# Down products of inner tiles 0 to 15 as seven quarter products, over sums of inner quarters

## The chip, the cores and the metric

The kernel runs on one core of one Trainium2 chip. The metric is the device time of one execution, in microseconds (us), the median of several runs. Its engines are called PE (matmuls; PEld are its weight loads), DVE, ACT, POOL and SP (which issues the weight DMAs).

## What is computed

Two transformer blocks in float32 on 512 tokens of width 1024. Three places are feed-forward networks (FFN) with an inner width of 2816, one in the first block and two in the second; everything between them (projections, attention, mixers) is left as it is by this change.

```python
def first_block(...):
    ...
    hn = rms_norm(h, norm2_g)
    gate, up = jnp.split(hn @ w_gate_up, 2, axis=-1)
    h = h + (jax.nn.silu(gate) * up) @ w_down        # FFN 0
    return rms_norm(h, final_g)[:, N_META:]
def second_block(...):
    x = x + 0.5 * swiglu(rms_norm_2(x, ffn1_norm), w_gate, w_up, w_down)   # FFN 1
    ...
    x = x + 0.5 * swiglu(rms_norm_2(x, ffn2_norm), w_gate, w_up, w_down)   # FFN 2
    x = x + sigmoid(rms_norm_2(x, ple_norm) @ w_ple_gate) * (p @ w_ple_proj)
```

## The kernel before

Activations lie transposed: the 1024 channels are 8 tiles of 128 partitions, the 512 tokens are columns. A float32 product is made of three float32r passes, high x high, high x low and low x high (`passes`, L791). So each weight chunk (`raw`, up to 128x2048) is split: ACT writes the rounded high part (`whi`), POOL the rest (`wlo`), both in two slots, and activations have high and low parts as well (`xh`, `xl`; inner ones `fh`, `fl`, a ring of 9 tiles).

An FFN is a line of 34 chunks (`PLACES`): "up" chunks, one for each of the 22 inner tiles (gate and up weights for 128 inner channels), and "down" chunks, four in each of three rounds r, each adding to two output tiles of `hT`. The rounds take 6, 8 and 8 inner tiles (`DOWN_K`) and stand behind 7, 8 and 7 up chunks (`UPS`). The places are called p = 0 to 33 here.

Up chunks of inner tiles 4 to 21 are folded (`fold_chunk`, L932): the 2x2 block product (two halves of the 1024 inputs, gate and up columns, two halves of the tokens) is made with seven quarter products of 256 columns instead of eight, which is 7 x 4 x 3 = 84 matmuls of 256 columns in place of 48 of 512. The seven, P0 to P6 in the order in which PE runs them, need sums of weight quarters (`corner_sums`, `sums_low`, on DVE, through PSUM banks 1, 3, 5, 7), sums of activation quarters (`fsh`, `fsl`, made once an FFN by `fold_sums`) and copies of partial results between them: ACT's three `kept` copies (`prod_kept`) before P2, P3 and P4, DVE's `up_done` additions before P5 and P6. Down chunks are plain: `down_chunk`, L975, 3 matmuls of 512 columns for each inner and output tile.

Everything is ordered by hand. Each engine has its own `ffn(f, ...)` loop over p and waits on counting semaphores. In place p, ACT makes the high parts of chunk p+1 (`coming`, in four steps between its other work), POOL their low parts, DVE finishes chunk p-1 and adds up chunk p+1's quarters. In the last round each finished output tile is fed to the next norm at once (`feed`): ACT scales and squares it (L1355, L1363, for FFN 0 a second square, L1373, since a norm with the final gain follows first), DVE writes the low part (`split`) and adds the squares (`add_square`, L1907, and L1915). POOL's loop, whose order matters for the change, is in its core

```python
for p in range(1, FFN_LEN):
    if folded(p + 1):
        fold_low(f, p + 1)
        continue
    ...
    if p + 1 < FFN_LEN:
        low(C_F[f] + p + 1)
```

and begins an FFN with `low(C_F[f])` and `low(C_F[f] + 1)`, the low parts of its first two chunks. A plain chunk on PE waits for its own `low` (`w_lo`), and the first chunk after an FFN waits for the squares' sum between its matmuls (`norm_sums`, L897; for FFN 1 between its two output tiles).

Of the kernel before, what the change touches and what calls it, by code (L numbers as in the profile page):

```python
# [47 lines left out]
DOWN_K = (6, 8, 8)  # L48
UPS = (7, 8, 7)
# [78 lines left out]

def folded(p):

    return up_tile(p) is not None and up_tile(p) >= PLAIN


def fold_no(f, p):

    return (FK - PLAIN) * f + up_tile(p) - PLAIN
# [22 lines left out]
def build(nc, I, out):  # L159
    with ExitStack() as ctx:  # L160
# [50 lines left out]
        fsh = at("fsh", 0, [P, 4, 4 * FOLD + 8], F32R)[:, :, 0:4 * FOLD].rearrange("p n (k t) -> p n k t", k=4)  # L211
        fsl = at("fsl", 4128, [P, 4, 4 * FOLD + 8], F32R)[:, :, 0:4 * FOLD].rearrange("p n (k t) -> p n k t", k=4)
        fh = at("fh", 8320, [P, RING, T], F32R)
        fl = at("fl", 12928, [P, RING, T], F32R)
        foldh = at("foldh", 17536, [P, 6, 4 * P + 8], F32R)[:, :, 0:4 * P].rearrange("p (s u) n -> p s u n", s=2)
        foldl = at("foldl", 20656, [P, 6, 4 * P + 8], F32R)[:, :, 0:4 * P].rearrange("p (s u) n -> p s u n", s=2)
        tmp = at("tmp", 23808, [P, 4, T])
        low_sum = at("low_sum", 25856, [P, 4, P])
        prod1 = at("prod1", 26368, [P, FOLD])
        prod5 = at("prod5", 26624, [P, FOLD])  # L220
        prod6 = at("prod6", 26880, [P, FOLD])
# [121 lines left out]
        silu_done, h_done, h_hi, h_split = sem("silu_done"), sem("h_done"), sem("h_hi"), sem("h_split")  # L343
# [84 lines left out]
        def corner(n, a, b):  # L428

            return raw[:, n % 2, :].rearrange("p (k n) -> p k n", k=DK)[:, 4 * a:4 * a + 4, P * b:P * b + P]  # L430
# [5 lines left out]
        def unit(c, n):  # L436

            if n < 4:
                return whi[:, c % 2, 4 * P * n:4 * P * n + 4 * P], wlo[:, c % 2, 4 * P * n:4 * P * n + 4 * P]
            return foldh[:, c % 2, n - 4, :], foldl[:, c % 2, n - 4, :]  # L440
# [4 lines left out]
        def fold_out(c):  # L445

            return ps[:, bank(c, 0), FOLD:T], ps[:, bank(c, 1), 0:FOLD], ps[:, bank(c, 1), FOLD:T]

# [8 lines left out]
        def _(sp):  # L457
# [26 lines left out]
            def ffn(f, gate, up, down):  # L484
                for p in range(FFN_LEN):
                    c = C_F[f] + p
                    if up_tile(p) is not None:
                        s, sel = slot(c, DK, CW), slice(P * up_tile(p), P * up_tile(p) + P)
                        load(c, [(s[:, :, 0:P], gate[:, :, sel]), (s[:, :, P:CW], up[:, :, sel])])
                    else:  # L490
# [120 lines left out]
        def _(pool):  # L611
# [49 lines left out]
            def ffn(f):  # L661
                low(C_F[f])
                low(C_F[f] + 1)
                for p in range(1, FFN_LEN):
                    if folded(p + 1):
                        fold_low(f, p + 1)
                        continue
# [1930 lines left out]
```

## Time and profile before

| what | us |
|---|---|
| median of 3 runs (lowest, highest) | 1967.1 (1965.23, 1967.56) |
| the profiled execution, its own time | 1966.0 |
| its span, first to last instruction | 1964.2 |
| PE busy | 1946.3 (99%) |
| DVE, POOL, ACT busy | 1197.6, 1134.5, 931.3 |
| share of PE in the chain that ended last | 88% |

Each row of the timeline below gives start, duration, engine, line, operation, output<-input, shapes and count; in brackets the time for which the engine had waited and for whom. A matmul's duration covers its way through the pipeline, so the pace of PE is read from starts and from stretches, not from durations. The 128x512 in a row is partitions x columns.

### The profile page before, as it was taken

Reading aid. Unit: us, or ns where it says so; the run is one execution under the profiler, and the core shown is the slowest. Engines: PE = TensorE matmul, PEld = TensorE weight load, DVE = VectorE, ACT = ScalarE, POOL = GpSimd, SP = SyncE. Lnnn points to the kernel's source line nnn. Section 1 sums busy time; section 2 is a strip of 40 time slices with the busy share of each in tenths; the row PEclk is TensorE's granted clock in tenths of the full one; section 3 lists DMA queues with packets and bytes.
Section 4 is the critical chain, followed back from the end, with each engine's and each line's share of the span. In section 5 each row is a group of like instructions: output and inputs, shape, how many; then the busy total and the mean of one; then the engine's idle time right before and its main releaser. Section 6 shows DMA issues by size and latency. Waiting matters only on the chain.

```text
span 1964.2 us, 30689 instructions
## 1 busy us (share of the span) xinstructions
PE 1946.3 (99%) x11449; PEld 1719.8 (88%) x11449; DVE 1197.6 (61%) x2067; ACT 931.3 (47%) x1649; POOL 1134.5 (58%) x915
## 2 busy tenths in 40 slices
PE   9999999999999999999999999999999999999999
PEld 8998887888899989879998988889888888999977
DVE  6588665635647455775755656677645565646574
ACT  6413225533536435454552644667644463634532
POOL 5344442254667657557775756666554566766663
PEclk9999999999999999999999999999999999999999
DMA  5222331123333333323333332332222333333331
GB/s 179 91 87 91 102 94 56 44 86 107 87 108 103 113 86 108 102 71 108 108 108 88 107 108 87 107 101 79 77 89 86 94 94 106 106 113 91 108 109 75
DMA packets 253850, 189.68 MB, mean 97 GB/s; under 512 B 6608, under 2 KB 249680, under 8 KB 253680
## 3 DMA queue, kind: packets, MB, share of 16 engines
q1 hardware_dynamic: 253024, 187.53, 32.0%
q8 instruction: 87, 1.43, 0.3%
q14 instruction: 51, 0.42, 0.1%
q10 hardware_dynamic: 688, 0.31, 0.1%
HBM read 180.93 MB, written 2.10 MB: 93 GB/s over the span
## 4 chain that ended last, share of the span: by engine, by line
PE 88%; DVE 5%; ACT 3%; issue 3%; POOL 1%; DMA 0%; DVEq 0%; SPq 0%; ACTq 0%
PE ps L793 18%; PE ps L794 18%; PE ps L795 18%; PE ps L944 9%; PE ps L945 9%; PE ps L946 9%; PE ps L1133 1%; PE ps L1285 1%; DVE tmp L1891 1%; ACT whi L1350 1%; PE ps L1205 1%; PE ps L1206 1%; PE ps L1207 1%; DVE hT L2076 1%; PE ps L1273 1%
## 5 line engine op out<-in xcount | busy, mean ns | idle before, releaser
L631 POOL TENSOR_TENSOR wlo<-raw,whi 128x512 fp32r<-128x512 f32 (+2 forms) x420 | 547.2, 1335 | 532.2 <-ACT whi L1350 411.3
L793 PE MATMUL ps<-xh,whi 128*128 128x512 f32 (+1 forms) x1008 | 380.3, 377 | 1.7 <-POOL wlo L631 1.7
L795 PE MATMUL ps<-xh,wlo 128*128 128x512 f32 (+1 forms) x1008 | 372.9, 370 | 0.0
L794 PE MATMUL ps<-xl,whi 128*128 128x512 f32 (+1 forms) x1008 | 372.7, 370 | 0.0
L1350 ACT ACTIVATE whi<-raw 128x2048 fp32r<-128x2048 f32 (+1 forms) x86 | 160.8, 1869 | 335.5 <-PE ps L795 287.1
L654 POOL TENSOR_TENSOR wlo<-raw,whi 128x512 fp32r<-128x512 f32 x162 | 213.2, 1318 | 152.6 <-ACT whi L1404 152.4
L793 PEld LDWEIGHTS ps<-xh,whi 128*128 128x128 f32 x1008 | 189.5, 188 | 33.4 <-POOL wlo L631 2.5
L795 PEld LDWEIGHTS ps<-xh,wlo 128*128 128x128 f32 x1008 | 189.3, 188 | 33.0
L794 PEld LDWEIGHTS ps<-xl,whi 128*128 128x128 f32 x1008 | 189.9, 188 | 28.4 <-issue 0.7
L793 PE MATMUL ps<-fh,whi 128*128 128x512 f32 x528 | 205.9, 390 | 1.6 <-POOL fl L643 1.6
L794 PE MATMUL ps<-fl,whi 128*128 128x512 f32 x528 | 205.6, 389 | 0.0
L795 PE MATMUL ps<-fh,wlo 128*128 128x512 f32 x528 | 205.4, 389 | 0.0
L1404 ACT ACTIVATE whi<-raw 128x512 fp32r<-128x512 f32 x162 | 102.0, 633 | 160.0 <-PE ps L946 102.4
L2001 DVE TENSOR_TENSOR foldl<-ps,foldh 128x512 fp32r<-128x512 f32 x162 | 108.2, 688 | 31.0 <-ACT foldh L1408 29.9
L944 PE MATMUL ps<-fsh,whi 128*128 128x256 f32 x432 | 121.7, 282 | 3.4 <-ACT prod L1462 3.4
L946 PE MATMUL ps<-xh,wlo 128*128 128x256 f32 x432 | 122.0, 282 | 0.0
L945 PE MATMUL ps<-xl,whi 128*128 128x256 f32 x432 | 121.9, 282 | 0.0
L944 PE MATMUL ps<-xh,whi 128*128 128x256 f32 x432 | 121.9, 282 | 0.0
L946 PE MATMUL ps<-fsh,wlo 128*128 128x256 f32 x432 | 121.5, 281 | 0.0
L945 PE MATMUL ps<-fsl,whi 128*128 128x256 f32 x432 | 121.5, 281 | 0.0
L944 PE MATMUL ps<-fsh,foldh 128*128 128x256 f32 x432 | 121.4, 281 | 0.0
L946 PE MATMUL ps<-fsh,foldl 128*128 128x256 f32 x432 | 121.4, 281 | 0.0
(385 smaller groups left out, 4900.1 us busy)
## 6 DMA issues: line engine op xcount, KB each, us to landing
raw<-in_w_in SPq DMA_DIRECT2D x87, 512.0 KB, 4.5
raw<-in_w_gate_up SPq DMA_DIRECT2D x44, 512.0 KB, 5.0
raw<-in_ffn_w_gate SPq DMA_DIRECT2D x44, 512.0 KB, 4.0
raw<-in_ffn_w_up SPq DMA_DIRECT2D x44, 512.0 KB, 5.3
raw<-in_ffn_w_down SPq DMA_DIRECT2D x32, 512.0 KB, 4.3
raw<-in_w_down SPq DMA_DIRECT2D x16, 512.0 KB, 4.1
raw<-in_ffn_w_down SPq DMA_DIRECT2D x16, 384.0 KB, 3.4
raw<-in_w_b SPq DMA_DIRECT2D x8, 512.0 KB, 3.9
```

The source lines that it names most:

```text
L631: ins = pool.tensor_tensor(wlo[:, c % 2, cs], raw[:, c % 2, cs], whi[:, c % 2, cs].bitcast(F32), ALU.subtract)
L654: pool.tensor_tensor(by_k(lo), corner(c, a, b), by_k(hi).bitcast(F32), ALU.subtract).then_inc(raw_lo, 1)
L793: pe.matmul(o, w_of(whi), xhi, start=first, stop=False)
L794: pe.matmul(o, w_of(whi), xlo, start=False, stop=False)
L795: return pe.matmul(o, w_of(wlo), xhi, start=False, stop=last)
L944: pe.matmul(o, wh[:, ks], hi[:, k, :], start=first and k == 0, stop=False, skip_group_check=True)
L945: pe.matmul(o, wh[:, ks], lo[:, k, :], start=False, stop=False, skip_group_check=True)
L946: mm = pe.matmul(o, wl[:, ks], hi[:, k, :], start=False, stop=k == 3, skip_group_check=True)
L1133: mm = pe.matmul(o[:, first:T], ctok[:, q, :], pT[:, q, first:T], start=q == 0, stop=False)
L1350: act.activation(whi[:, c % 2, 0:n], raw[:, c % 2, 0:n], ACT.Copy).then_inc(w_hi, 1)
L1404: act.activation(by_k(unit(c, u)[0]), corner(c, a, b), ACT.Copy).then_inc(raw_hi, 1)
L2001: dve.tensor_tensor(lo, ps[:, 3 + 2 * m, :], hi.bitcast(F32), ALU.subtract).then_inc(sum_lo, 1)
```

## The change

- `DOWN_K` becomes 8, 8, 6 and `UPS` 9, 8, 5: rounds 0 and 1 now take eight inner tiles each (0 to 15), behind one more up chunk than they need, and round 2 takes the last six.
- The eight down chunks of rounds 0 and 1 are folded too: 84 matmuls of 256 columns over inner tiles 2i (first half) and 2i+1 (second half) and the two halves of the tokens. Round 2 stays plain, with 36 matmuls of 512 columns a chunk instead of 48.
- New sums of inner quarters, for each pair of tiles i = 0 to 7, in two stages (`f_sums`, `f_lows` on DVE, `f_forms` on ACT), at the places that `FORM_STEPS` gives: one stage in each of two places, except i = 3 and i = 7, whose two stages stand in one place (p = 8 and p = 20). Their high and low parts lie in `fs24h`, `fs24l` and in halves of `fh`, `fl`, `xh`, `xl` that are free; SP moves one of them by two small DMAs.
- In an up chunk the addition `up_done` is made once, behind P4, and in PSUM; the inner tile is then made from PSUM in two halves. `low_sum`, `prod1`, `prod6` are gone (their places are `raw` itself and `tmp`).
- The quarter sums of weights use bank 3 twice, so that bank 7 is free for the inner sums; the third now waits for the first one's low part.
- The update of `hT` reads the scaled product from PSUM, not from `tmp`.
- FFN 1: the multiplication of `hT` by the final gain and norm, on DVE in round 0 before, is made by ACT (`gain_done`) and POOL (`xn_done`) in places 3 to 10.
- FFN 0, round 2: seven of the eight additions of squares go from DVE to POOL.

```diff
-DOWN_K = (6, 8, 8)
-UPS = (7, 8, 7)
+DOWN_K = (8, 8, 6)
+UPS = (9, 8, 5)
...
+    return up_tile(p) is not None and up_tile(p) >= PLAIN or down_part(p) is not None and down_part(p)[0] < 2
...
+FORM_STEPS = {}
+for _i in range(DK):
+    _p = UP_AT[2 * _i + 1] + 1
+    FORM_STEPS.setdefault(_p, []).append((_i, 0))
+    FORM_STEPS.setdefault(_p if _i % 4 == 3 else _p + 1, []).append((_i, 1))
...
@@ gpsimd, ffn
+                    if f == 0 and down_part(p) is not None:
+                        for m in fed(p):
+                            pool.wait_ge(sq_done, 2 * DK + m + 1)
+                            pool.wait_ge(ssum_done, 19 + m)
+                            pool.tensor_tensor(ssum[:, META:TM], ssum[:, META:TM], sq[:, META:TM], ALU.add).then_inc(ssum_done, 1)
...
@@ vector, ffn
+            def f_sums(f, i, stage):
+
+                a, b, s = slice(0, FOLD), slice(FOLD, T), ps[:, 7, :]
+                dve.wait_ge(fs_lo, form_level(f, i, stage) - 1)
+                if stage == 0:
+                    dve.wait_ge(acc_free, 2 * (C_F[f] + UP_AT[2 * i + 1]) + 2)
+                    dve.tensor_tensor(s[:, a], f_t[0][:, a], f_t[1][:, a], ALU.add)
+                    dve.tensor_tensor(s[:, b], f_t[0][:, b], f_t[0][:, a], ALU.subtract).then_inc(fs_sum, 1)
+                else:
+                    link(dve.tensor_tensor(s[:, b], s[:, b], f_t[1][:, a], ALU.subtract))
+                    dve.tensor_tensor(s[:, a], s[:, b], f_t[1][:, b], ALU.add).then_inc(fs_sum, 1)
...
+                    for i, stage in steps[:1]:
+                        f_sums(f, i, stage)
                     if new:
+                        sums_low(f, p + 1, 0)
                         corner_sums(f, p + 1, 2)
-                        sums_low(f, p + 1, 0)
+                    for i, stage in steps[:1]:
+                        f_lows(f, i, stage)
+                    for i, stage in steps[1:]:
+                        f_sums(f, i, stage)
+                    if new:
                         sums_low(f, p + 1, 1)
...
-                        dve.wait_ge(prod_done, 5 * m + 4)
-                        dve.wait_ge(prod_kept, 3 * m + 3)
-                        dve.wait_ge(h_done, FK * f + up_tile(p))
-                        dve.tensor_tensor(tmp[:, 2, FOLD:T], r5, prod6[:], ALU.add).then_inc(up_done, 1)
+                        dve.wait_ge(prod_done, 5 * m + 5)
+                        dve.wait_ge(prod_kept, 3 * m + 2)
+                        dve.tensor_tensor(fold_up(c), r1, prod5[:], ALU.add).then_inc(up_done, 1)
...
-                        stt(tmp[:, 2, :], ps[:, bank(c, t), :], factor, rsx, ALU.mult, ALU.mult).then_inc(acc_free, 1)
-                        dve.tensor_tensor(x, x, tmp[:, 2, :], ALU.add).then_inc(h_new, 1)
+                        link(stt(o, o, factor, rsx, ALU.mult, ALU.mult))
+                        link(dve.tensor_tensor(x, o, x, ALU.add))
+                        feed(S + 1, m, gain, own_square=not (S + 1 == 2 and m < DK - 1))
```

POOL at the end of FFN 0 and the start of FFN 1 (`wlo<-raw,whi` is the low part of a chunk, `fl` that of an inner tile, `ssum<-ssum,sq` an addition of squares). Before, from the last inner tile's low part in FFN 0 on:

```order
136 L631 TENSOR_TENSOR wlo<-raw,whi 128x512 x4
137 L643 TENSOR_TENSOR fl<-tmp,fh 128x512 x2
138 L631 TENSOR_TENSOR wlo<-raw,whi 128x512 x24
139 L643 TENSOR_TENSOR fl<-tmp,fh 128x512
140 L631 TENSOR_TENSOR wlo<-raw,whi 128x512 x4
```

After:

```order
162 L704 TENSOR_TENSOR wlo<-raw,whi 128x384 x4
163 L717 TENSOR_TENSOR fl<-rt,fh 128x512
164 L717 TENSOR_TENSOR fl<-sq,fh 128x512
165 L704 TENSOR_TENSOR wlo<-raw,whi 128x384 x4
166 L759 TENSOR_TENSOR ssum<-ssum,sq 128x512
167 L704 TENSOR_TENSOR wlo<-raw,whi 128x384 x4
168 L759 TENSOR_TENSOR ssum<-ssum,sq 128x512 x2
169 L704 TENSOR_TENSOR wlo<-raw,whi 128x384 x4
170 L759 TENSOR_TENSOR ssum<-ssum,sq 128x512 x4
171 L704 TENSOR_TENSOR wlo<-raw,whi 128x512 x12
```

The seven additions stand between the low parts of the down chunks; the last four, for output tiles 3 to 6, stand ahead of row 171, whose first four are the low part of FFN 1's first chunk.

DVE in one folded up chunk, p = 8 of FFN 0, where both stages of i = 3 stand (`ps<-rt,sq`, `ps<-rt`, `ps<-ps,sq` are the sums, `xl<-ps,xh`, `fl<-ps,fh` and `fs24l` their low parts; `ps<-ps,prod` is the addition for which P6 waits). Before, a folded up chunk was:

```order
592 L2013 TENSOR_TENSOR tmp<-ps,rs 128x256
593 L1988 TENSOR_TENSOR ps<-ps,raw 128x512
594 L1991 TENSOR_TENSOR ps<-ps,raw 128x512
595 L2023 TENSOR_TENSOR tmp<-tmp 128x512
596 L1994 TENSOR_TENSOR ps<-ps,raw 128x512
597 L2001 TENSOR_TENSOR foldl<-ps,foldh 128x512 x2
598 L2041 TENSOR_TENSOR tmp<-ps,prod_59 128x256
599 L2001 TENSOR_TENSOR foldl<-ps,foldh 128x512
600 L2045 TENSOR_TENSOR tmp<-ps,prod_58 128x256
```

After, from the inner tile's product on:

```order
656 L2194 TENSOR_TENSOR sq<-tmp,ps 128x256
657 L2195 TENSOR_TENSOR sq<-tmp,ps 128x256
658 L2121 TENSOR_TENSOR ps<-rt,sq 128x256
659 L2122 TENSOR_TENSOR ps<-rt 128x256
660 L2158 TENSOR_TENSOR sum_l<-ps,sum_h 128x512
661 L2151 TENSOR_TENSOR ps<-ps,raw 128x512
662 L2133 TENSOR_TENSOR xl<-ps,xh 128x256
663 L2133 TENSOR_TENSOR fl<-ps,fh 128x256
664 L2124 TENSOR_TENSOR ps<-ps,sq 128x256
665 L2125 TENSOR_TENSOR ps<-ps,sq 128x256
666 L2158 TENSOR_TENSOR sum_l<-ps,sum_h 128x512
667 L2229 TENSOR_TENSOR ps<-ps,prod_60 128x256
```

Six new operations of 256 columns stand ahead of row 667.

## Rows read from the trace of the kernel before

**Rows 1.** The page: span, busy time, granted clock in tenths by slice.

```profile
span 1964.2 us, 30689 instructions
...
PE 1946.3 (99%) x11449; PEld 1719.8 (88%) x11449; DVE 1197.6 (61%) x2067; ACT 931.3 (47%) x1649; POOL 1134.5 (58%) x915
...
PEclk9999999999999999999999999999999999999999
```

**Rows 2.** Stretches of FFN 0: from:to us, then length, busy us (count) of each engine.

```profile
531.94:561.84 29.90, 29.90 (x253) 29.89 (x252) 14.47 (x27) 15.83 (x34) 20.46 (x17) 1.00 0.36 107
...
594.51:674.75 80.24, 79.98 (x674) 79.80 (x672) 51.18 (x91) 46.42 (x97) 59.28 (x47) 1.00 0.38 107
...
674.75:718.29 43.54, 43.54 (x194) 36.04 (x193) 18.69 (x22) 11.85 (x14) 24.07 (x18) 1.00 0.32 99
```

**Rows 3.** Timeline of PE: the longest wait at a folded chunk.

```profile
951.86 0.35 PE L944 MATMUL ps<-fsh,whi 128*128 128x256 f32 x1 [2.41 <-ACT prod L1462]
```

**Rows 4.** Waits of PE from 480 us on: for whom, us, times, longest.

```profile
PE ps L944 <- ACT prod L1462: 3.4, 6, 2.4
PE ps L910 <- DVE ssl L1926: 2.6, 2, 1.3
PE ps L793 <- POOL wlo L631: 1.7, 2, 1.0
```

**Rows 5.** Timeline: FFN 0's last tiles and the first chunk of FFN 1.

```profile
822.28 1.92 ACT L1350 ACTIVATE whi<-raw 128x2048 fp32r<-128x2048 f32 x1
...
824.28 4.85 POOL L631 TENSOR_TENSOR wlo<-raw,whi 128x512 fp32r<-128x512 f32 x3 [4.41 <-ACT whi L1350]
...
826.20 1.77 DVE L1907 TENSOR_TENSOR ssum<-ssum,sq 128x512 f32<-128x512 f32 x1
...
829.09 1.74 POOL L631 TENSOR_TENSOR wlo<-raw,whi 128x512 fp32r<-128x512 f32 x1
...
829.60 0.68 DVE L1891 SCALAR_TENSOR_TENSOR tmp<-ps,rs 128x512 f32<-128x512 f32 x1
...
832.05 0.62 ACT L1363 ACTIVATE sq<-hT 128x512 f32<-128x512 f32 x1
...
832.92 0.68 DVE L1907 TENSOR_TENSOR ssum<-ssum,sq 128x512 f32<-128x512 f32 x1
...
832.90 0.39 PE L793 MATMUL ps<-xh,whi 128*128 128x512 f32 x1
...
841.23 0.79 PE L793 MATMUL ps<-xh,whi 128*128 128x512 f32 x1
```

**Rows 6.** Timeline: FFN 2's last round and the chunk behind it.

```profile
1859.32 0.40 PE L793 MATMUL ps<-fh,whi 128*128 128x512 f32 x1
...
1864.81 0.50 PE L793 MATMUL ps<-fh,whi 128*128 128x512 f32 x1 [0.54 <-POOL fl L643]
...
1903.75 0.39 PE L793 MATMUL ps<-xh,whi 128*128 128x512 f32 x1
...
1912.71 0.50 PE L910 MATMUL ps<-ssh,ones 128*128 128x512 f32 x1 [1.32 <-DVE ssl L1926]
```

**Rows 7.** Groups by line: busy us, mean ns of one.

```profile
L652 POOL TENSOR_TENSOR low_sum<-raw 128x512 f32<-128x512 f32 x54 | 70.6, 1307 | 0.0
...
L631 POOL TENSOR_TENSOR wlo<-raw,whi 128x384 fp32r<-128x384 f32 x48 | 52.1, 1116 | 38.1 <-ACT whi L1350 28.3 <-ACT whi L1395 9.8
```

**Rows 8.** Timeline: DVE and ACT in a folded chunk that PE begins at 634.80.

```profile
639.71 0.40 ACT L1462 ACTIVATE prod<-ps 128x256 f32<-128x256 f32 x1
...
640.78 0.43 DVE L2041 TENSOR_TENSOR tmp<-ps,prod 128x256 f32<-128x256 f32 x1 [0.63 <-PE ps L946]
```

**Rows 9.** Timeline: FFN 1, places 2 to 4.

```profile
869.99 0.50 PE L793 MATMUL ps<-xh,whi 128*128 128x512 f32 x1 [0.98 <-POOL wlo L631]
...
880.92 0.68 DVE L2056 TENSOR_TENSOR tmp<-ps,rs 128x512 f32<-128x512 f32 x1
...
882.66 0.39 ACT L1462 ACTIVATE prod<-ps 128x256 f32<-128x256 f32 x1 [0.28 <-PE ps L946]
```

More of the change, by code:

```diff
@@ L935, in fold_chunk, with product @@
                 r1, r5, r2 = fold_out(c)
-                k1, k2 = slice(0, 4), slice(4, DK)
-                late = slice(META + FOLD, TM)
-                early = slice(META, META + FOLD)
-                def product(o, u, hi, lo, first=True, last=True):
-                    wh, wl = unit(c, u)
+                late, early = slice(FOLD, T), slice(0, FOLD)
+                part = down_part(p)
+                def product(o, u, rows, first=True):
+                    wh, wl = unit(f, p, u)
                     for k in range(4):
@@ L943, in product @@
                         ks = slice(P * k, P * k + P)
[L944 to L950 removed]
+                        hi, lo = rows(k)
@@ new lines, in product, with form, quarter, rows @@
+                        pe.matmul(o, wh[:, ks], hi, start=first and k == 0, stop=False, skip_group_check=True)
+                        pe.matmul(o, wh[:, ks], lo, start=False, stop=False, skip_group_check=True)
+                        mm = pe.matmul(o, wl[:, ks], hi, start=False, stop=k == 3, skip_group_check=True)
+                    return mm
+                def form(m):
+                    return lambda k: x_form(m, k) if part is None else f_form(part[0], m, k)
+                def quarter(second, half):
+                    def rows(k):
+                        if part is None:
+                            cs = slice(META + half.start, META + half.stop)
+                            return xh[:, 4 * second + k, cs], xl[:, 4 * second + k, cs]
+                        z = (DK * part[0] + 2 * k + second) % RING
+                        return fh[:, z, half], fl[:, z, half]
+                    return rows
@@ new lines, in ffn @@
+                    kept(tmp[:, 0, 0:FOLD], r1, 3)
+                    for i in FORMS_AT[f == 1].get(p, ()):
+                        x_forms(f, i, own)
+                    steps = FORM_STEPS.get(p, [])
+                    for i, stage in steps[:1]:
+                        f_forms(f, i, stage)
+                    coming(3)
+                    for i, stage in steps[1:]:
+                        f_forms(f, i, stage)
+                    if f == 1 and p - PLAIN + 1 in range(DK):
+                        m = p - PLAIN + 1
+                        act.wait_ge(fs_sum, form_level(f))
+                        act.activation(hT[:, m, META:TM], hT[:, m, META:TM], ACT.Copy, scale=col(vec, V_FIN + m)).then_inc(gain_done, 1)
```

344 lines of the change are left out of this document (220 added, 124 removed).

## The prediction

> **What bounds the kernel now.** I read the page first. PE is busy for 1946.3 of 1964.2 us and its granted clock is full in all forty slices [rows 1]; no other engine is above 61%. So the time is PE's: the matmuls that it has, at their pace, and its few waits. The stretches of FFN 0 give the pace: three folded chunks 29.90, eight 80.24, four plain down chunks with eight inner tiles 43.54 [rows 2]. That is 9.97 to 10.03 for a folded chunk and 10.885 for a plain one. Then the list of PE's waits: 3.4 us in six waits for ACT's copy `prod`, one of them 2.41, each in the first folded chunk after a down round [rows 3, 4]; the rest are small. The reader is to see that a change can gain only PE time or these waits, and that DVE (6.4 us in a folded up chunk of 10.03), ACT (5.8) and POOL (7.4) have a third or less to spare before they set the pace themselves [rows 2].
>
> The profiled execution took 1966.0, 1.1 below the median of 1967.1. I sum changes against it and apply the same sum to the median.
>
> **1. Cheaper matmuls.** Each FFN had four down chunks with six tiles and eight with eight; now eight with eight tiles are folded and four with six are plain. So 24 chunks go from 10.885 to 9.99 us, 84 matmuls of 256 columns for 48 of 512: 24 x 0.895 = **-21.5**. This is certain as long as PE is fed.
>
> **2. Waits that go.** No folded chunk follows a plain down chunk any more, and the scaling of `hT` in FFN 1 leaves DVE's round 0, behind which the 2.41 stood. All six waits go: **-3.4** [rows 3, 4]. At the low end none but the 2.41 goes.
>
> **3. DVE inside a folded down chunk.** Its work is two updates of `hT` of two operations each, six sums, the addition before P6 and one more of 512 columns. In steps of 0.6 to 0.7 us for 512 columns and 0.4 for 256 (the 0.43 and 0.68 of [rows 8, 5]) this is about 8 us of 9.99. It fits, and PE's P6 waits for an addition that can start, as now, 0.3 us behind P4's end, 1.42 us ahead of P6. ACT's third copy ends at 640.11, PE wants it at 634.80 + 4 x 1.42 = 640.5 [rows 8]; new work stands behind it. Price 0 in the steady case, hidden by that slack of 0.4; what it costs without it is the slower rival.
>
> **4. Both stages of i = 3 and i = 7 in one place.** In an ordinary up chunk the new sums add four operations of 256 columns ahead of the addition for P6, about 1.7 us, or 2.7 where the two with both inputs in SBUF run beside POOL. DVE had some 3 us idle [rows 2], and by my count the addition is ready 0.6 us early. In p = 8 and p = 20 six operations stand there, and it is 0.3 to 0.4 late. 6 x 0.35 = **+2.1**, between 0 and 6 x 1 us.
>
> **5. Start of FFN 1.** Its activation sums are made in places 1 and 2, so DVE is late: the gate product of place 3 starts at 880.92, and ACT's copy in the first folded chunk is made at 882.66, 1.2 us ahead of need (883.87, PE's third product) [rows 9]. The stages (0,0) and (0,1) put about 2.4 and 1.6 us ahead of that product, 1.1 of idle time goes, and ACT's new scaling adds 0.5. The copy comes at 885.7: **+1.9**, between 0 and 3. FFN 0 and 2 begin less densely and have some 3 us to spare there. The 0.98 wait [rows 9] stays.
>
> **6. End of FFN 1 and FFN 2.** Round 2 is shorter by 4 x 2.72 = 10.9 us on PE, but not on DVE. From its start to the norm's matmul was 1912.71 - 1859.32 = 53.39 [rows 6]; with 10.9 less it would be 42.5. Now follow DVE. The last inner tile's low part ended 5.49 us behind the round's start [rows 6]; ACT's shorter high part ahead of it saves 0.3, and the first output tile is done at 5.9 (4.08 without the wait, which was 0.54 and is now 1.8). Each output tile then costs DVE: product 0.72, update 0.73, 0.83 until ACT's high part is there, low part 0.67, addition 0.60, together 3.55. Beside POOL the last two take 1.1 and 1.7, 5.1 in all; one tile of each two is so, since POOL has four operations of 1.1 for each chunk [rows 7], and the addition shows both times, 1.77 and 0.68 [rows 5]. Two tiles are 8.65 against PE's 8.16. Eight tiles from 6.1 on, with 0.8 of early waits, end at 41.5, the split of the sum (3.1) at 44.6. That is 2.1 over 42.5, **+4.2** for both, between 2 and 7.
>
> POOL, by the Trainium skill (GPSIMD Engine Reference, 1. Specifications), shares its SBUF interfaces with DVE, and contends with DVE instructions that have two SBUF inputs. The trace agrees: 1.77 beside POOL, 0.68 without. It speaks for the updates of `hT`, which read PSUM now, and against the additions that move to POOL.
>
> **7. End of FFN 0.** Here is the largest loss. DVE gives seven additions of squares to POOL, where the last four stand ahead of the low part of FFN 1's first chunk. Today ACT has that chunk's high part ready at 824.20, POOL lowers it from 824.28 to 830.83, PE needs it at 832.90 [rows 5]: 2.07 us of cover. In the new order POOL cannot begin before it has added the square of output tile 6. When is that? DVE's tile costs product and update 1.45, then it waits for ACT's second square (scale, square, square: 1.9 us behind the update), then the second sum's addition, 0.6 alone and up to 1.7 beside POOL, which now adds in just that moment: 3.95 to 5.05, and I take 4.9. PE's tile takes 4.08. Tile 6's product starts at 6.1 + 6 x 4.9 = 35.5 behind the round's start, its square is there 3.07 later (829.60 to 832.67) [rows 5], 38.6, POOL's addition takes 1.3 [rows 7], 1.6 beside DVE, 40.2, the low part 5.2 to 6.5 [rows 5, 7], say 6.3: 46.5. PE has ended the round at 34.5, so it waits 12.0. Add 0.9 for the wait at the round's start as in 6, take off 1.0 for waits inside that chunk (832.90 to 841.23 is 8.33 us [rows 5]) that have been served by then: **+11.9**. With 3.95 a tile it is 6.5; with every operation slow, 14.5.
>
> **8. After an idle time of 12 us.** The longest idle time in the rows is 2.41, and behind it a matmul took 0.35 in place of 0.28 [rows 3]; at that the clock stayed full [rows 1]. What 12 us do is not shown. Bounds: nothing, or the whole next pass of 24 matmuls of 0.227 at the lower level of 1.2 GHz, twice the time, 5.4. I take **+2.0**, nearer to the row.
>
> Sum: -21.5 - 3.4 + 2.1 + 1.9 + 4.2 + 11.9 + 2.0 = **-2.8** or, with the roundings, -2.9. That is 1963.1 for an execution like the profiled one and **1964.2 for the median**.
>
> **The rivals.**
>
> A. The boundary behind FFN 0 costs no more than the other two (2.1), because DVE and ACT run closer to 3.95 a tile and POOL finds time early. For it: 2.07 us of cover today [rows 5]. Against: the order has no way around, tile 6's square comes after the moment at which the low part now begins. -2.8 - 9.8 - 2.0 = -14.6, 1952.5.
>
> B. The clock falls in the 12 us and takes its whole price, 5.4 in place of 2.0: +3.4, 1967.6. The rows neither show nor exclude it. The Trainium skill (TensorE: Matmul & The Clock Gate, The HAM clock gate) says that the array falls to half rate after an idle window and must be busy to get back; by that rule part of the following pass is slow, and no row here has such an idle time.
>
> C. Slower than before: the folded chunk no longer fits DVE and ACT. Place: ACT's third copy ahead of P4, 0.4 us of slack [rows 8]. In a folded down chunk DVE ends its second update of `hT` about 0.65 behind the next chunk's first need, ACT's sums wait for DVE's, and the copy waits behind them. From 0.4 more on, PE waits in each of the 24 chunks; with 0.5 each it is +12, 1976.2. Against it: round 2's operations on PSUM and the sums show 0.6 to 0.7 each, and my count leaves 0.4.
>
> **How the numbers follow.** Forecast 0.52, A 0.16, B 0.17, C 0.15. About 0.2%, 3.9 us, is what a measurement of this kernel can tell from no change. The forecast's own range is 1957 to 1970, with the ends of terms 4 to 8 set against each other, and its middle lies near the border at 1963.2: 0.24 faster, 0.27 the same, 0.01 slower. A is faster. B gives 0.02 faster, 0.13 the same, 0.02 slower. C is slower. Sum: faster 0.42, same 0.40, slower 0.18. The range takes in the forecast, B, part of A and of C: 1955 to 1974.
>
> **What would show it.** A folded down chunk's 84 matmuls at 10.0 us and no waits in the steady ones (1, 3). In p = 8 and 20 a wait of some 0.3 at P6 for DVE (4). In FFN 1's p = 4 a wait at the third product for ACT (5). Norm sums of the last two FFNs 44.6 behind the round's start (6). One wait of PE of about 12 us for `wlo` at FFN 1's first chunk, with four additions of `ssum` in front on POOL, and the granted clock behind it (7, 8). I am wrong if that wait is under 6 us, or if PE waits in most folded down chunks.

## The result, and the profile after

The changed kernel takes **2095.9 us** (median of 4 runs, 2090.7 to 2099.2) against 1967.0 of the kernel before: 1.0655 times as long, 95% interval 1.0643 to 1.0668. The prediction was 1964.2, range 1955 to 1974, with 0.18 on slower. It was wrong by 132 us, nearly all of it in one term.

The page of the changed kernel, to be read beside [rows 1]: PE was busy for 99% of the span and is for 94% now. Of the chain of work that ended last, PE had 88% before; it has 69% now, and DVE and ACT have 24%.

```profile
span 2088.6 us, 33448 instructions
...
PE 1953.5 (94%) x12313; PEld 1758.1 (84%) x12313; DVE 1372.0 (66%) x2412; ACT 1042.3 (50%) x1951; POOL 1156.0 (55%) x954
...
PE 69%; DVE 17%; ACT 7%; issue 6%; POOL 1%; DMA 0%; DVEq 0%; ACTq 0%; SPq 0%; POOLq 0%
```

PE's waits in the changed kernel, for whom, us in total, times, longest. They answer to [rows 4]:

```profile
PE ps L1030 <- ACT tmp L1578: 107.2, 76, 3.0
PE ps L879 <- POOL wlo L704: 12.4, 3, 11.1
PE ps L879 <- POOL fl L717: 4.6, 3, 1.5
PE ps L879 <- DVE xl L2025: 1.8, 2, 1.5
PE ps L996 <- DVE ssl L2061: 1.7, 2, 0.8
...
PE ps L1030 <- DVE ps L2229: 0.3, 2, 0.2
```

The first row is new and is nearly everything: 76 waits in 78 folded chunks, the up chunks that were folded already among them, nearly all of them before P4 for ACT's third kept copy (L1578). The other rows are about what was forecast. The stretches of FFN 0, to be read beside [rows 2] (from:to, length, busy us of PE, PEld, DVE, ACT, POOL, granted clock):

```profile
531.83:837.38 305.55, 270.25 (x2185) 265.95 (x2184) 210.85 (x355) 160.72 (x339) 186.18 (x149) 0.98 0.32 91
837.38:883.21 45.83, 33.20 (x146) 26.78 (x144) 31.41 (x37) 25.27 (x32) 30.09 (x25) 0.93 0.24 70
```

26 folded chunks take 305.55 us, 11.75 each, where 26 x 9.99 = 259.7 were expected. With FFN 1 (304.1) and FFN 2 (303.1) that is 133 us too much, more than the whole loss of 124.4 between the two spans.

**Why the copy is late.** The changed kernel in the folded down chunk whose P4 PE starts at 625.13 (start, duration, engine, line, operation; in brackets how long the engine had waited, and for whom), ACT and PE first, then DVE:

```profile
622.02 0.60 ACT L1516 ACTIVATE sum_h<-ps 128x512 fp32r<-128x512 f32 x1 [0.20 <-DVE ps L2148]
624.11 0.60 ACT L1516 ACTIVATE sum_h<-ps 128x512 fp32r<-128x512 f32 x1 [1.49 <-DVE ps L2151]
624.61 0.38 ACT L1578 ACTIVATE tmp<-ps 128x256 f32<-128x256 f32 x1
...
625.13 0.35 PE L1030 MATMUL ps<-fh,whi 128*128 128x256 f32 x1 [0.90 <-ACT tmp L1578]
```

```profile
622.65 0.69 DVE L2158 TENSOR_TENSOR sum_l<-ps,sum_h 128x512 fp32r<-128x512 f32 x1 [0.66 <-ACT sum_h L1516]
623.38 0.70 DVE L2151 TENSOR_TENSOR ps<-ps,raw 128x512 f32<-128x512 f32 x1
```

Read the two as one line. ACT makes the high part of the first sum (622.02). DVE waits for it, writes its low part (622.65), then makes the third sum (623.38), and only then ACT may make the high part of the *second* sum (624.11): `sum_high(m)` waits for `3 * n + min(m + 2, 3)` sums, which for m = 1 is all three. The kept copy is queued behind it. In the kernel before, the third sum stood ahead of the first low part and ended at 638.25, before ACT came to its second copy, so ACT made both in one go (new rows, of before, for the chunk of [rows 8]):

```profile
637.56 0.69 DVE L1994 TENSOR_TENSOR ps<-ps,raw 128x512 f32<-128x512 f32 x1
...
638.24 1.08 ACT L1408 ACTIVATE foldh<-ps 128x512 fp32r<-128x512 f32 x2
```

The diff exchanged these two lines on DVE, since bank 3 holds the first sum until its low part is made and the third sum now goes there. It left ACT's wait as it was.

**Where it is 2.7 us.** In an up chunk in which stage 0 stands, DVE is late as well (changed kernel, DVE, then ACT and PE):

```profile
678.32 1.54 DVE L2121 TENSOR_TENSOR ps<-rt,sq 128x256 f32<-128x256 f32 x1
679.78 1.52 DVE L2122 TENSOR_TENSOR ps<-rt 128x256 f32<-128x256 f32 x1
681.21 0.68 DVE L2158 TENSOR_TENSOR sum_l<-ps,sum_h 128x512 fp32r<-128x512 f32 x1
681.92 0.70 DVE L2151 TENSOR_TENSOR ps<-ps,raw 128x512 f32<-128x512 f32 x1
```

```profile
682.65 0.60 ACT L1516 ACTIVATE sum_h<-ps 128x512 fp32r<-128x512 f32 x1 [3.11 <-DVE ps L2151]
...
684.19 0.36 PE L1030 MATMUL ps<-xs13h,whi 128*128 128x256 f32 x1 [2.73 <-ACT tmp L1578]
```

Two sums of 256 columns take 1.5 us each; stage 1's, of the same size but with one operand in PSUM, take 0.43. I had priced both at some 0.95, and only in p = 8 and 20 did I count their delay.

### The profile page after: what moved, and what is told of

Read it like the earlier page. It is cut to its first block, busy times and chain, and to the rows that moved or that the text cites. A ratio compares the mean times of both kernels' runs of the same rounds, so it can differ in the third digit from the quotient of the medians.

```text
span 2088.6 us, 33448 instructions
## 1 busy us (share of the span) xinstructions
PE 1953.5 (94%) x12313; PEld 1758.1 (84%) x12313; DVE 1372.0 (66%) x2412; ACT 1042.3 (50%) x1951; POOL 1156.0 (55%) x954
## 4 chain that ended last, share of the span: by engine, by line
PE 69%; DVE 17%; ACT 7%; issue 6%; POOL 1%; DMA 0%; DVEq 0%; ACTq 0%; SPq 0%; POOLq 0%
PE ps L879 13%; PE ps L880 12%; PE ps L881 12%; PE ps L1030 8%; PE ps L1032 8%; PE ps L1031 8%; DVE ps L2025 2%; DVE ps L2151 2%; DVE sum_l L2158 2%; DVE ps L2145 2%; ACT fh L1600 2%; DVE ps L2122 1%; DVE ps L2121 1%; ACT tmp L1578 1%; PE ps L1239 1%
## 5 line engine op out<-in xcount | busy, mean ns | idle before, releaser
L704 POOL TENSOR_TENSOR wlo<-raw,whi 128x512 fp32r<-128x512 f32 (+2 forms) x324 | 410.0, 1297 | 428.8 <-ACT whi L1456 330.6
L730 POOL TENSOR_TENSOR wlo<-raw,whi 128x512 fp32r<-128x512 f32 x234 | 303.5, 1298 | 345.2 <-ACT whi L1510 345.2
L1510 ACT ACTIVATE whi<-raw 128x512 fp32r<-128x512 f32 x234 | 147.9, 632 | 174.7 <-PE ps L1032 174.0
L1516 ACT ACTIVATE sum_h<-ps 128x512 fp32r<-128x512 f32 x234 | 140.2, 599 | 154.9 <-DVE ps L2151 150.0
L2158 DVE TENSOR_TENSOR sum_l<-ps,sum_h 128x512 fp32r<-128x512 f32 x234 | 159.8, 684 | 68.8 <-ACT sum_h L1516 68.8
L1030 PE MATMUL ps<-xs13h,whi 128*128 128x256 f32 x216 | 66.0, 306 | 82.1 <-ACT tmp L1578 82.1
L728 POOL TENSOR_TENSOR raw<-raw 128x512 f32<-128x512 f32 x78 | 104.7, 1342 | 0.0
L830 POOL TENSOR_TENSOR wlo<-raw,whi 128x384 fp32r<-128x384 f32 (+1 forms) x84 | 75.6, 931 | 51.4 <-ACT whi L1920 50.7
L1030 PE MATMUL ps<-fh,whi 128*128 128x256 f32 x288 | 83.1, 289 | 22.1 <-ACT tmp L1578 22.1
L735 POOL TENSOR_TENSOR wlo<-raw,whi 128x512 fp32r<-128x512 f32 x78 | 101.1, 1296 | 0.0
L1030 PE MATMUL ps<-xh,sum_h 128*128 128x256 f32 x312 | 88.2, 283 | 0.6 <-DVE ps L2229 0.3
```

What stands on the lines that cost most here:

```text
L704: ins = pool.tensor_tensor(wlo[:, c % 2, cs], raw[:, c % 2, cs], whi[:, c % 2, cs].bitcast(F32), ALU.subtract)
L730: pool.tensor_tensor(by_k(lo), corner(f, p, a, b), by_k(hi).bitcast(F32), ALU.subtract).then_inc(raw_lo, 1)
L1030: pe.matmul(o, wh[:, ks], hi, start=first and k == 0, stop=False, skip_group_check=True)
L1510: act.activation(by_k(unit(f, p, u)[0]), corner(f, p, a, b), ACT.Copy).then_inc(raw_hi, 1)
L1516: act.activation(unit(f, p, 4 + m)[0], ps[:, (3, 5, 3)[m], :], ACT.Copy).then_inc(sum_hi, 1)
L2158: dve.tensor_tensor(lo, ps[:, (3, 5, 3)[m], :], hi.bitcast(F32), ALU.subtract).then_inc(sum_lo, 1)
```

## The experiments

All compared with the kernel before on the same chip, in three rounds. A diff is against the changed kernel unless it says otherwise, and "+ e1" means that the edit stands on top of experiment 1.

### 1. Both copies together

```diff
-                    act.wait_ge(corner_sum, 3 * n + min(m + 2, 3))
+                    act.wait_ge(corner_sum, 3 * n + (2, 2, 3)[m])
...
                     dve.wait_ge(sum_lo, 3 * n + 1)
+                    dve.wait_ge(sum_hi, 3 * n + 2)
                     dve.tensor_tensor(sums(3), sums(5), corner(f, p, 1, 0), ALU.add).then_inc(corner_sum, 1)
```

> The changed kernel; ACT's second copy of a sum no longer waits for the third sum, and DVE's third sum waits for that copy instead (so bank 5 is still read by one engine at a time). Theory A (ACT's third kept copy is late because the copy ahead of it waits behind DVE's low part and third sum): the wait of 0.9 or 2.7 us before P4 goes in nearly all of the 78 folded chunks; 107 us of listed waits and some 20 of what they bring behind them go, 1965 to 1985 us. DVE's addition before P6 may now be the next to be late in the chunks with stage 0. Theory B (DVE as a whole is too full in chunks with stage 0, the copy is only where it shows): the 0.9 waits go, the 24 of 2.7 us move to P6 at about 2 us each: 2010 to 2030. Theory C (the folded chunk is slower for another reason, the waits are filled by something else): above 2060.

Measured: **1966.2 us**, ratio 1.0002 (0.9992 to 1.0011). Two waits moved, and 130 us are gone: theory A. The time is 2 us above the 1964.2 that I had forecast for the change; how far that is luck is said below. PE's waits in this kernel:

```profile
PE ps L879 <- POOL wlo L704: 12.4, 3, 11.1
PE ps L1030 <- DVE ps L2230: 6.9, 7, 1.0
PE ps L879 <- POOL fl L717: 4.6, 3, 1.5
...
PE ps L1030 <- ACT tmp L1578: 1.2, 1, 1.2
```

ACT's copy is late once, at FFN 1's start. DVE's addition before P6 is now late 1.04 us in each p = 8 and p = 20, six times, which the waits before P4 had covered in the changed kernel (0.17 twice).

The second wait is there so that ACT's copy and DVE's third sum don't read bank 5 together. No run here shows what would come of that; the Trainium skill (PSUM — Partial Sum Buffer, PSUM bank collisions raise a hardware error) says that two engines may not touch one bank at once, reads included.

### 2. The exchange alone, in the kernel before

```diff
@@ the kernel before
-                        corner_sums(f, p + 1, 2)
                         sums_low(f, p + 1, 0)
+                        corner_sums(f, p + 1, 2)
                         sums_low(f, p + 1, 1)
```

> The kernel before with one thing of the change alone: DVE makes the low part of the first sum ahead of the third sum, not behind it. Theory A: ACT's second copy of a sum waits for both, about 2 us later than now, its third kept copy ends near 1.2 us behind PE's need, in each of 54 folded chunks: +65 to +80, 2030 to 2050 us. If the order of these two is not the cause: within 5 us of the kernel before.

Measured: **2027.9 us**, ratio 1.031 (1.030 to 1.033). The exchange of two lines costs the kernel before 62 us, with nothing else of the change in it:

```profile
PE ps L944 <- ACT prod L1462: 51.9, 45, 4.7
```

It is a little under the expected 2030: I had counted 54 chunks, and the list has 45. The last chunk of each of the nine runs of folded ones has no such wait, since no folded chunk follows it whose sums DVE and ACT would have to prepare in it.

### 3. The third copy first

```diff
                     coming(2)
+                    kept(tmp[:, 0, 0:FOLD], r1, 3)
+                    coming(4)
                     if n is not None:
...
-                    kept(tmp[:, 0, 0:FOLD], r1, 3)
```

`coming(2)` makes only the first sum's high part here, and a new step, `coming(4)`, the second's.

> The changed kernel; only ACT's order differs: its third kept copy stands ahead of the second copy of a sum and of the inner tile's high part, all waits as they were. Theory A: PE no longer waits before P4, about 1965 to 1985 us, close to the kernel in which the two copies stand together. Theory B: as there, 2010 to 2030. If ACT's amount of work were the cause, not the wait in front of the copy, then the copy would be as late as before in the chunks without a wait and the time would stay above 2060.

Measured: **2024.2 us**, ratio 1.028 (1.027 to 1.030). A miss. The wait before P4 went in all steady chunks, so ACT's amount of work was not the cause; but it came back at P6 in the chunks with stage 0. ACT's second copy still waits 2.17 us for DVE's third sum, and what stands behind it on ACT, stage 0's two copies, is late for DVE, in whose queue the addition for P6 stands behind them (DVE, then PE):

```profile
672.24 0.42 DVE L2135 TENSOR_TENSOR xl<-ps,xh 128x256 fp32r<-128x256 f32 x1 [1.73 <-ACT fh L1552]
672.58 0.41 DVE L2135 TENSOR_TENSOR fl<-ps,fh 128x256 fp32r<-128x256 f32 x1
672.91 0.68 DVE L2160 TENSOR_TENSOR sum_l<-ps,sum_h 128x512 fp32r<-128x512 f32 x1
673.51 0.42 DVE L2231 TENSOR_TENSOR ps<-ps,prod 128x256 f32<-128x256 f32 x1
```

```profile
674.08 0.42 PE L1030 MATMUL ps<-xh,sum_h 128*128 128x256 f32 x1 [1.94 <-DVE ps L2231]
```

So moving the late copy forward treats the place where the wait shows. Only taking away the detour over DVE (1) helps.

### 4. Stage 0 with one operand from PSUM

```diff
-                    dve.tensor_tensor(s[:, a], f_t[0][:, a], f_t[1][:, a], ALU.add)
-                    dve.tensor_tensor(s[:, b], f_t[0][:, b], f_t[0][:, a], ALU.subtract).then_inc(fs_sum, 1)
+                    dve.tensor_tensor(s[:, a], s[:, a], f_t[1][:, a], ALU.add)
+                    dve.tensor_tensor(s[:, b], s[:, b], f_t[0][:, a], ALU.subtract).then_inc(fs_sum, 1)
```

> The changed kernel; the two sums of stage 0 read one operand from PSUM (bank 7) in place of the one in SBUF, so the sums of inner quarters are not the right ones; count, shapes and order of all instructions are kept. Theory: the price of 1.54 and 1.52 us is that of two operands in SBUF beside POOL's work; with one in PSUM each takes about 0.42, the wait before P4 in the 24 chunks with stage 0 falls from 2.7 to about 0.9: -45 to -50, 2045 to 2055 us, while the waits of 0.9 stay. Rival: POOL's work slows any operation of DVE at that place: they stay near 1.5 and the time near 2096.

Measured: **2052.1 us**, ratio 1.043 (1.042 to 1.045).

```profile
PE ps L1030 <- ACT tmp L1578: 76.1, 75, 3.0
```

The 18 waits of 2.73 us are 1.11 now, the 0.9 waits stay. So with the detour in place stage 0's two operands in SBUF cost some 44 of the 129 us (31 of them in the list of waits, some 9 in the clock behind long waits, below). The two shares don't simply add: experiment 1 takes away the detour alone and gets all 130 back, since without it the same slow sums mostly fit into DVE's slack.

### 5. What makes two operands in SBUF slow: POOL's instruction in halves (+ e1)

```diff
                     pool.wait_ge(raw_hi, 3 * n + z + 1)
-                    pool.tensor_tensor(by_k(lo), corner(f, p, a, b), by_k(hi).bitcast(F32), ALU.subtract).then_inc(raw_lo, 1)
+                    for k in (slice(0, 2), slice(2, 4)):
+                        ins = pool.tensor_tensor(by_k(lo)[:, k], corner(f, p, a, b)[:, k], by_k(hi)[:, k].bitcast(F32), ALU.subtract)
+                    ins.then_inc(raw_lo, 1)
```

> The kernel with both copies together (e1); POOL makes the low parts of the first three weight quarters of a folded chunk in two instructions of 256 columns each in place of one of 512. In the trace of e1 the two sums of stage 0 (256 columns, 1.54 and 1.53 us) end 0.3 us behind POOL's two operations that run at that time (574.27 for 1.29, 575.51 for 1.49). Theory L: DVE's operation with two operands in SBUF does not run slowly beside POOL's, it waits for the end of POOL's instruction and then takes 0.3. Then the first of the two falls to about 1.0 or less, the waits of 1.04 at P6 shrink or go: 1959 to 1963. Theory S: the two share the memory's ports by the element, and an instruction's length doesn't matter: both stay near 1.5 us, and the time at 1966 or, as POOL's own work grows by some 0.7 a chunk, up to 1 above.

Measured: **1956.3 us**, ratio 0.9947 (0.9930 to 0.9964), 9.9 below experiment 1, although POOL has more to do. In quarters (four slices of one k each):

> The kernel with both copies together (e1), with POOL's low parts of the first three weight quarters in four instructions of 128 columns each. Theory L (DVE's operation with two operands in SBUF waits for the end of POOL's running instruction): the first sum of stage 0, 1.54 us beside instructions of 512 columns and 0.99 beside those of 256, is near 0.7 here. If instead a halved POOL instruction merely let DVE in after a fixed time, it stays at 0.99. The time: as e7, 1956 to 1958, or higher by what POOL's greater work costs, since a quarter's low part then takes some 1.9 us and P3 waits for it if that is late.

Measured: 1963.0 us (1959.6 to 1966.2), ratio 0.9982 (0.9973 to 0.9992). The same place, the end of p = 8's inner tile in FFN 0, with POOL's instructions whole, halved and quartered (experiment 1, then 5, then quarters; DVE's sum and POOL's instructions beside it):

```profile
574.31 1.54 DVE L2121 TENSOR_TENSOR ps<-rt,sq 128x256 f32<-128x256 f32 x1
...
574.27 1.29 POOL L730 TENSOR_TENSOR wlo<-raw,whi 128x512 fp32r<-128x512 f32 x1 [0.47 <-ACT whi L1510]
```

```profile
574.06 0.99 DVE L2123 TENSOR_TENSOR ps<-rt,sq 128x256 f32<-128x256 f32 x1
...
574.02 1.62 POOL L731 TENSOR_TENSOR wlo<-raw,whi 128x256 fp32r<-128x256 f32 x2 [0.34 <-ACT whi L1512]
```

```profile
573.62 0.72 DVE L2123 TENSOR_TENSOR ps<-rt,sq 128x256 f32<-128x256 f32 x1
...
572.24 3.44 POOL L731 TENSOR_TENSOR wlo<-raw,whi 128x128 fp32r<-128x128 f32 x7
```

One POOL instruction takes 1.29, 0.75 and 0.47 us (the means of these groups over the FFNs are 1297, 750 and 470 ns), DVE's sum 1.54, 0.99 and 0.72: each time 0.25 more than POOL's. The ends say it more sharply: of the 48 sums of stage 0 in each of these three traces 40, 38 and 42 took over 0.5 us, and every one of them ended 0.29 or 0.30 us behind the end of a POOL instruction; the others, with POOL idle or just ending, took 0.42 to 0.50. The sum does not run slowly beside POOL; it stands still until a POOL instruction ends, then does its own work. The Trainium skill says so (SBUF — State Buffer, SBUF: two separate sides): the port pair that DVE and POOL share is an exclusive lock held for a whole instruction, and a DVE operation with two SBUF inputs needs it where the POOL operation reads SBUF. The trace agrees, with these three pairs; I had cited a softer sentence of another page and priced a mean slowdown.

The gain of 9.9 is more than the six waits of 1.04. In experiment 1 the up chunks with stage 0 took 10.25 us and the others 9.91, a stop at P6 too short for the list of waits; in halves nearly all take 9.91. In quarters the steady chunks do too, but one wait of 3.9 us for DVE's addition stands in the list of the profiled run, and the runs spread over 6.5 us.

The trace shows what makes that wait, and halves have it as well. At one place, p = 6 of FFN 1, POOL has work without a pause, and DVE's sum is not let in behind the first of POOL's instructions but only behind the last (the kernel with halves, DVE, then POOL):

```profile
908.95 3.59 DVE L2123 TENSOR_TENSOR ps<-rt,sq 128x256 f32<-128x256 f32 x1
```

```profile
908.11 2.88 POOL L731 TENSOR_TENSOR wlo<-raw,whi 128x256 fp32r<-128x256 f32 x4
910.89 1.36 POOL L728 TENSOR_TENSOR raw<-raw 128x512 f32<-128x512 f32 x1
```

Four POOL instructions end while the sum stands, and it takes 3.59 us; in quarters, at the same place, ten do and it takes 5.73. With whole instructions POOL waited for ACT between them there, and the sum took 1.54. PE's wait for the addition behind it is 1.06 in halves and 3.87 in quarters. The whole 6.7 us between the two kernels are not explained by that, as only one execution of each was profiled. Nor is it shown what decides whether DVE is let in between two POOL instructions: elsewhere it was, between two halves without a pause too.

### 6. Stage 1 behind the addition (+ e1)

```diff
-                    for i, stage in steps[1:]:
-                        f_sums(f, i, stage)
-                    if new:
+                    if new and not steps[1:]:
                         sums_low(f, p + 1, 1)
...
                         dve.tensor_tensor(fold_up(c), r1, prod5[:], ALU.add).then_inc(up_done, 1)
+                        for i, stage in steps[1:]:
+                            f_sums(f, i, stage)
+                        if new and steps[1:]:
+                            sums_low(f, p + 1, 1)
```

> The kernel with both copies together (e1); in the two places of an FFN where both stages stand, DVE makes the addition that P6 waits for ahead of stage 1's two sums and of the second low part. Theory: the six waits of 1.04 us at P6 go with the 0.2 each that follows them, -6 to -7.5, about 1959 us. Rival: the operations that move behind the addition make the next chunk's first kept copy or its silu late; then up to 1 us of each comes back, 1962 to 1966.

Measured: **1962.3 us**, ratio 0.9978 (0.9968 to 0.9987), 3.8 below experiment 1. That is the lower end of the rival's range, and for the rival's reason: the six waits of 1.04 at P6 went, and six of 0.29 for ACT's first copy of the next chunk came.

### 7. The boundary behind FFN 0 (+ e1)

The low part ahead of POOL's additions for tiles 4, 5 and 6:

```diff
-                        for m in fed(p):
+                        for m in {FFN_LEN - 2: (3,), FFN_LEN - 1: (4, 5, 6)}.get(p, fed(p)):
+                            if m == 4:
+                                low(C_F[1])
```

> The kernel with both copies together (e1), and POOL makes the low part of FFN 1's first chunk ahead of the additions for output tiles 4, 5 and 6, not behind all seven. Theory (PE's 11.07 us at the boundary are the way round POOL's additions): POOL starts the low part when ACT's high part is there, 825.2 in the trace of e1, and has it near 831, against PE's need at 828.4, so that wait is 2 to 3 us; the sum of squares then comes late instead, at 841 to 843, where PE wants it near 838.5, 2 to 4 us. Saving 5 to 7: 1959 to 1961.5. Rival: the boundary is held by DVE's output tiles (4.7 to 5.0 us each), whose last low part PE needs as well; then the 11 us come back in other waits and the time stays within 2 us of 1966.

Measured: **1965.8 us**, ratio 0.9998 (0.9988 to 1.0007): nothing gained, the rival. The low part stands ready 9 us earlier and PE's wait for it is 1.93; then PE waits 3.19 and 4.30 for `xl`, the low parts of the last output tiles. The reason is on ACT, which can't feed the next tile until POOL has added tile 4's square, behind the low part:

```profile
825.47 4.99 POOL L704 TENSOR_TENSOR wlo<-raw,whi 128x512 fp32r<-128x512 f32 x4 [4.12 <-ACT whi L1459]
830.42 1.29 POOL L762 TENSOR_TENSOR ssum<-ssum,sq 128x512 f32<-128x512 f32 x1
...
831.79 0.72 ACT L1464 ACTIVATE xh<-hT,vec 128x512 fp32r<-128x512 f32 x1 [6.40 <-POOL ssum L762]
```

All three edits (1, 6 and this one) in one kernel:

> Both copies together, the low part ahead of the squares, and stage 1 behind the addition, all three in one kernel: if their savings add, 1966.2 - 5.5 - 7 = 1953.7, 1951 to 1957, which is faster than the kernel before by 0.5 to 0.8%. If the time that one saves is taken back at the other's place it is 1958 or more.

Measured: 1961.5 us, ratio 0.9975 (0.9964 to 0.9985). Since the low part's new place gives nothing, the sum is that of 6 alone. The part of the change undone, all squares on DVE again:

```diff
-                        feed(S + 1, m, gain, own_square=not (S + 1 == 2 and m < DK - 1))
+                        feed(S + 1, m, gain, own_square=True)
```

> The kernel with both copies together (e1), with one part of the change undone: in the last round of FFN 0 DVE adds all squares itself, POOL none. The chunk's low part is then not behind POOL's additions, and the 11.07 us wait for it goes. Theory (the boundary is a chain of eight output tiles on ACT and DVE, 4.7 us each, as the kernel with the low part moved ahead showed, where the 11 us came back as waits for the tiles' low parts): DVE's tile becomes 1.3 to 1.7 longer, the last low part comes near 845 to 849, the waits are for xl instead, 10 to 14 us in all, and the time is 1965 to 1970. If the low part's place alone held PE, about 1955 to 1957.

Measured: 1963.8 us, ratio 0.9985 (0.9975 to 0.9994), 2.4 below experiment 1. That lies between the two expectations, nearer the first. PE's waits at this place are now 0.44 and 3.25 for `wlo` and 3.75 for `xl`, 7.4 in place of 11.07: a third of it is gained, a third is now the tiles' chain, and a third is still low parts of chunks. So handing the squares to POOL was not worth anything here.

### 8. The low part in pieces between the additions (+ 1 and 5)

POOL was idle for 3.4 us ahead of each addition. The low part is cut into eight pieces of 256 columns, four ahead of tile 5's addition and four ahead of tile 6's:

```diff
                         for m in fed(p):
+                            if p == FFN_LEN - 1:
+                                c = C_F[1]
+                                pool.wait_ge(w_hi, c + 1)
+                                for z in range(4):
+                                    cs = slice(256 * (4 * (m - 5) + z), 256 * (4 * (m - 5) + z) + 256)
+                                    ins = pool.tensor_tensor(wlo[:, c % 2, cs], raw[:, c % 2, cs], whi[:, c % 2, cs].bitcast(F32), ALU.subtract)
+                                if m == 6:
+                                    ins.then_inc(w_lo, 1)
```

> The kernel with POOL's halves (e7), and the low part of FFN 1's first chunk is made in eight pieces of 256 columns: four ahead of the addition for tile 5, four ahead of that for tile 6. POOL stood idle for 3.4 us ahead of each of these additions in the trace of e1, and four pieces take about 2.9, so the additions are not later by more than 0.5 and the tiles keep their pace. The chunk is ready near 4 us behind the round's end in place of 11.07; the last tiles' low parts (837 and 838.3 in e1's time) and the sum (841.7, 4.9 ahead of PE's use of it in e1) then hold PE. Saving 4 to 5: 1951 to 1952.5 against 1956.3 of e7. Rival: POOL's pieces stand in DVE's way (its operations with two operands in SBUF wait for them) and the tiles become slower: saving under 2.

Measured: **1950.2 us** (1950.05 to 1950.28), ratio 0.9917 (0.9900 to 0.9933). It is 6.2 below experiment 5's kernel, a little more than the 4 to 5 expected, and the fastest of the study, 0.8% faster than the kernel before. PE's wait for the chunk's low part is 5.49 us in place of 11.08, where I had expected some 4. What is left on PE:

```profile
PE ps L890 <- POOL wlo L765: 5.5, 1, 5.5
PE ps L890 <- POOL fl L717: 4.6, 3, 1.5
PE ps L890 <- DVE xl L2036: 1.8, 2, 1.5
```

POOL's two other instructions of a folded chunk in halves too:

> As the kernel with the pieces (e10), and POOL's two other instructions in a folded chunk (the difference of two weight quarters, and the low part of it) are in halves as well. The second sum of stage 0 ran beside that difference and took 0.97 us in e7; it falls to some 0.85. No wait of PE hangs on it but one of 1.06 in FFN 1, so the time is within 1.5 us of e10; POOL's further 0.3 us a chunk has room.

Measured: 1951.5 us, ratio 0.9926 (0.9909 to 0.9942), no better, as expected. The second sum of stage 0 did not get shorter (0.97), and at p = 6 of FFN 1 the first one stood through seven POOL instructions, 4.58 us in place of 3.56; PE's wait behind it is 2.05 in place of 1.03. There is a point from which smaller instructions on POOL stop paying.

## Why the prediction was wrong, point by point

- **3, DVE inside a folded down chunk: this step failed.** It priced the new order at 0, "hidden by that slack" of 0.4 us of ACT's third copy, and said that "new work stands behind it". The new work does; a new *wait* stands ahead of it. I counted operations per engine and compared sums, 8 of 9.99 us (the count was right: DVE is busy for 7.80 us in such a chunk of the changed kernel), and never followed which sum ACT's second copy waits for, though [rows 8] put the copy 0.4 us from its need. The detour (low part 0.69, third sum 0.70, the hand-overs) delays that copy by 1.5 us. It costs 0.9 to 1.1 in a chunk without stage 0, and it is not confined to the 24 new chunks, since up chunks changed their order too. Experiment 2 shows that part alone (+62), experiment 1 the whole (-130).
- **4, both stages in one place: the term was mis-sized.** +2.1 was forecast, with 1.7 to 2.7 us for the new operations. In the changed kernel it hides behind the waits at P4, and makes 18 of them 2.73 in place of 1.11 (experiment 4, 44 us with what follows them). With the detour gone it is 6 x 1.04 in waits and short stops in the other stage 0 chunks, 9.9 us together by experiment 5, and 11.9 by the chunks' lengths in experiment 1: 12 of 10.26 and 6 of 11.19 where one without stage 0 takes 9.91. The price per sum was 1.54, not 0.95, for the reason of experiment 5.
- **Rival C** named the right place, ACT's copy ahead of P4, and the right side. Its reason (too much work on DVE in a folded down chunk) and its price (0.5 in 24 chunks) were wrong, and so its chance, 0.15, went with "my count leaves 0.4".
- **1, cheaper matmuls: right.** A folded down chunk took 11.11 us in the changed kernel with its 0.90 wait, and in experiment 1 the stretch of 26 folded chunks is 262.06 us, 10.08 each with two waits of 1.04 in it. 9.98 was the steady down chunk.
- **2, waits that go: right** in experiment 1: none of the six, the 2.41 among them [rows 3, 4], is in its list.
- **5, start of FFN 1: right.** +1.9 was forecast; experiment 1 has 1.20 at P2 for ACT's copy, then 0.68 at P6 for DVE.
- **6, end of FFN 1 and 2: right.** Norm sums 44.6 us behind the round's start were forecast, for +4.2 in both. The changed kernel has 45.13 and 43.88, experiment 1 has 45.12 and 43.83; over the 42.5 that is +4.0. The wait at the first tile, forecast as 1.8, is 1.54.
- **7, end of FFN 0: right.** 12.0 was forecast for the wait at FFN 1's first chunk, 11.09 measured, with the four additions in front. But it had a second owner behind it: experiment 7 shows that the tiles' chain holds PE nearly as long, which my sum left out. That didn't touch the time, only what a cure is worth.
- **8, the clock: right.** +2.0 was forecast. Behind the 11.09 us PE ran at half its clock for 4.00 us, nine matmuls of 0.43 in place of 0.23, which is 1.8. The row is from the changed kernel:

```profile
883.21:887.21 4.00, 4.00 (x9) 3.14 (x10) 2.19 (x2) 0.00 (x0) 4.00 (x3) 0.50 0.69 196
```

Experiment 1, which has every term but 3, takes 1966.2 where 1964.2 was forecast. That these lie so close is in part luck. Term 4 is 9.8 more than I had put down, and some 6 came back where I had put too little or nothing: a steady folded up chunk takes 9.91 us where it took 9.97 (54 chunks, 3.2); the six chunks that lost their waits had been 4.9 longer than the others, for waits of 3.4; and the boundary behind FFN 0 cost 11.0, not 11.9.

## What to carry to other kernels

When a change exchanges two lines on one engine, don't sum the engine's work: take each wait of the *other* engines on the counter that the two lines raise, write down at which of the two it is served before and after, and see what is queued behind it there. A copy that is 0.4 us from being late has no slack for a trip to another engine and back, which took 1.5 us here. And a wait that is removed is worth only the distance to the next owner: the low part that was ready 9 us earlier gained nothing until the chain of output tiles kept its pace too.

## What the runs showed of the hardware

- A DVE operation with two operands in SBUF, beside POOL's work on SBUF, waits for the end of a POOL instruction and ends 0.29 us behind it (experiment 5). Mostly it is the instruction that is running, so that what it costs is set by that one's length, 1.54, 0.99 or 0.72 us for the same sum, so cutting POOL's work into halves made the whole kernel faster by 9.9 us although POOL's own time for that group rose from 303.4 to 340.3 us. But it can be passed over: at one place, where POOL had no pause, four to ten short POOL instructions went by and the sum took 3.56 to 5.73 us, so smaller instructions help only as long as DVE is let in between them. The same sum with one operand in PSUM took 0.43 everywhere (experiment 4).
- PE's clock after waits of 2 to 3 us differs from one wait to the next. The changed kernel has 20 waits of 1.98 to 2.99 us in its folded chunks. Behind 14 the granted clock stayed full; behind six, at once or up to 1.6 us later, it stood at half, the 1.2 GHz level, for 3 to 6 us. The longest of these stretches, directly behind a wait of 2.73:

```profile
563.60:569.73 6.13, 6.12 (x29) 6.13 (x29) 2.99 (x6) 2.43 (x6) 3.76 (x3) 0.50 0.07 6
```

  That makes 100 matmuls at 0.213 us in place of 0.117, 9.6 us in this execution. In experiment 3 it was behind 13 of 18 waits of 1.94 to 2.98, some 200 matmuls and 19 us, so a third of what that kernel lost. Behind waits of 1.3 us or less it was never seen in the folded chunks of the kernels whose matmuls I went through one by one (before, after, experiments 1 to 4, halves), and the 2.41 of the kernel before kept the full clock [rows 3]. It fits that the changed kernel's runs spread over 8.5 us and those of before over 2.3, and that its mean granted clock is 0.992 in the fastest run and 0.987 in the slowest. The Trainium skill (TensorE: Matmul & The Clock Gate, What's actually happening) says that how many matmuls run slow at a kernel's start differs from run to run; by these two clocks it differs here as well.
- Each short wait of PE in a folded chunk cost some 0.2 us more than the list says: 11.11 us for a down chunk is 9.98 + 0.90 + 0.23. Of the 133 us too much in the folded stretches 107 are listed waits, 9.6 the clock, and the other 17, shared by 76 waits, are this.
